# A mixture-of-experts router rebuilt: plain float32 logits on un-normed transposed rows, one block ranked at a time

## The reference, cut to what matters

```python
h = rms_norm(x, norm_ffn[l])
logits = einsum('bld,de->ble', h, router_w) + router_b
top_v, top_i = lax.top_k(logits, 2)
gates = sum(one_hot(top_i, 8) * softmax(top_v)[..., None], axis=-2)
for e in range(8):
    out = out + gates[..., e:e+1] * swiglu(h, wg[e], wu[e], wd[e])   # 1024 -> 2816 -> 1024
x = x + out
```

## Time and profile before

| | |
|---|---|
| median of 3 runs | 1372.85 us (1372.64 to 1375.06) |
| profiled execution, its own time | 1368.11 us |
| its span, first to last instruction | 1366.3 us |
| busy share of the span: PE, DVE, ACT, POOL | 96%, 73%, 59%, 9% |
| mean granted TensorE clock | 0.986 |
| share of PE in the chain that ended last | 91% |

### The profile page before, as it was taken

One profiled execution on the slowest core, in us unless ns is written; L12 is line 12 of the kernel. 1 busy time (PEld: TensorE's weight loads), 2 busy tenths in 40 slices (PEclk: granted clock), 3 DMA queues, 4 the chain that ended last, 5 costly groups with the idle time before them and its releaser, 6 DMA issues.

```text
span 1366.3 us, 15856 instructions
## 1 busy us (share of the span) xinstructions
PE 1312.4 (96%) x6292; PEld 1110.3 (81%) x6293; DVE 1001.6 (73%) x999; ACT 805.5 (59%) x817; POOL 119.3 (9%) x163
## 2 busy tenths in 40 slices
PE   5999999999998999979999999999999999999995
PEld 5997788888887997868888888888888888888884
DVE  5977533333335777478888988888889888888994
ACT  5545333222224465447777777777777777777771
POOL 1070200000000072020000000000000000000150
PEclk9999999999999999879999999999999999999998
DMA  9225597333332125169999999999999999999991
GB/s 317 88 74 183 188 414 275 123 123 123 123 124 84 62 78 192 47 249 395 389 389 378 385 384 383 383 388 370 389 379 383 390 369 390 390 373 371 392 343 60
DMA packets 179201, 373.71 MB, mean 274 GB/s; under 512 B 7084, under 2 KB 59748, under 8 KB 179126
## 3 DMA queue, kind: packets, MB, share of 16 engines
q1 hardware_dynamic: 167878, 335.78, 67.7%
q0 software_dynamic: 9456, 34.75, 6.8%
q10 hardware_dynamic: 1792, 2.18, 0.4%
HBM read 345.85 MB, written 26.82 MB: 273 GB/s over the span
## 4 chain that ended last, share of the span: by engine, by line
PE 91%; DVE 4%; ACT 2%; issue 1%; DMA 1%; SPq 0%; POOL 0%; DVEq 0%; POOLq 0%; ACTq 0%
PE ps L342 28%; PE ps L344 28%; PE ps L343 28%; PE ps L1548 2%; PE ps L1395 1%; DVE ext L916 1%; DVE a_lo L924 1%; PE ps L1477 1%; DVE w_lo L322 1%; ACT ext L587 1%; DMA ext<-in_norm_mix 1%; PE ps L1319 1%; PE ps L1351 1%; PE ps L1554 1%; DVE ps L952 0%
## 5 line engine op out<-in xcount | busy, mean ns | idle before, releaser
L322 DVE TENSOR_TENSOR w_lo<-raw,w_hi 128x2048 fp32r<-128x2048 f32 x317 | 725.1, 2291 | 140.6 <-ACT w_hi L633 81.0
L633 ACT ACTIVATE w_hi<-raw 128x2048 fp32r<-128x2048 f32 x264 | 506.3, 1919 | 139.2 <-PE ps L344 138.1
L342 PE MATMUL ps<-w_hi,xT_hi 128*128 128x512 f32 x704 | 279.8, 397 | 1.4 <-DVE xT_lo L1030 1.4
L344 PE MATMUL ps<-w_hi,xT_lo 128*128 128x512 f32 x704 | 274.9, 390 | 0.0
L343 PE MATMUL ps<-w_lo,xT_hi 128*128 128x512 f32 x704 | 274.2, 389 | 0.0
L344 PEld LDWEIGHTS ps<-w_hi,xT_lo 128*128 128x128 f32 x704 | 132.1, 188 | 28.6
L342 PEld LDWEIGHTS ps<-w_hi,xT_hi 128*128 128x128 f32 x704 | 132.3, 188 | 27.3 <-DVE xT_lo L1030 1.6
L343 PEld LDWEIGHTS ps<-w_lo,xT_hi 128*128 128x128 f32 x704 | 132.4, 188 | 26.1
L342 PE MATMUL ps<-w_hi,a_hi 128*128 128x512 f32 x360 | 141.1, 392 | 5.1 <-DVE a_lo L1130 3.0
L344 PE MATMUL ps<-w_hi,a_lo 128*128 128x512 f32 x360 | 140.3, 390 | 0.0
L343 PE MATMUL ps<-w_lo,a_hi 128*128 128x512 f32 x360 | 140.2, 389 | 0.0
(11 more groups left out here) (192 smaller groups left out, 1525.4 us busy)
## 6 DMA issues: line engine op xcount, KB each, us to landing
raw<-in_moe_w_down SPq DMA_DIRECT2D x88, 1024.0 KB, 7.5
raw<-in_moe_w_gate SPq DMA_DIRECT2D x80, 1024.0 KB, 7.3
raw<-in_moe_w_up SPq DMA_DIRECT2D x80, 1024.0 KB, 7.3
raw<-in_w_in SPq DMA_DIRECT2D x12, 1024.0 KB, 9.5
x_rows<-ext POOLq DMA_DIRECT2D x6, 2048.0 KB, 24.8
raw<-in_dense_w_gate SPq DMA_DIRECT2D x11, 1024.0 KB, 5.3
raw<-in_dense_w_up SPq DMA_DIRECT2D x11, 1024.0 KB, 5.4
raw<-in_dense_w_down SPq DMA_DIRECT2D x11, 1024.0 KB, 5.0
```

The costliest lines, as they stand in the source:

```text
L322: dve.tensor_tensor(slot(w_lo, s), slot(raw, s), slot(w_hi, s).bitcast(F32), ALU.subtract)\
L342: pe.matmul(out, lh, rh, start=start, stop=False)
L344: return pe.matmul(out, ll, rh, start=False, stop=stop)
L633: act.activation(slot(w_hi, s), slot(raw, s), ACT.Copy).then_inc(hi_ready[s], 1)
```

## The change

- **Logits.** The transposes take x before the norm (`pe_xT`), ACT copies the first two blocks to SBUF and DVE the third (`xt`), with no split. The router's weights are multiplied by the norm's gain once (`rw`; the gain arrives with the other per-channel parameters, one more small load at the start). The logits are 8 plain float32 matmuls of 8 columns per block, and 1/rms comes in as a scalar when DVE adds the bias.
- **Order on PE.** The first block's transposes, then half of the third block's last `w_out` part, the second block's transposes, a quarter, the second block's logits, the last quarter, the third block's transposes, the logits of the first and third blocks, 14 transposes of the identity into a bank that nobody reads (`keep_warm`), the counting, 10 more of these, the gather.
- **Order on ACT and DVE.** Tiles 2 and 3 are split ahead of the second block's residual add, tiles 4 and 5 on ACT ahead of the gather; on DVE tile 4 comes behind the gathered rows and tile 5 behind the gates. The ranking is one call per block (`route`), with one comparison pair and one weight table (`side`). The one-hot comes ahead of the counts and `posb`, the maximum for the softmax, the exponentials and the gates behind them.
- **Start of expert 0.** Its first tile waits only for the first half of the gathered rows; the gather's second half waits for the counts to be read.

```diff
+LOGIT_ORDER = [1, 0, 2]
+LOGIT_BANK = [7, 6, 2]
...
-        rw_hi = place("rw_hi", KD * NE, F32R)
-        rw_lo = place("rw_lo", KD * NE, F32R)
+        rw = place("rw", KD * NE)
...
+        xt = place("xt", KD * TOK, offset=oh)
...
-        low = place("low", NE * NE, offset=s0 + 512)
+        side = place("side", 2 * NE * NE, offset=s0 + 4096)
...
-        cmp_gt = place("cmp_gt", NTB * NE * NE, offset=s0 + 1024)
-        cmp_eq = place("cmp_eq", NTB * NE * NE, offset=s0 + 1792)
+        cmp = place("cmp", 2 * NTB * NE * NE, offset=s0 + 1024)
...
+        PRM_ROWS.append((C_NF, a["norm_ffn"][LAYERS - 1].rearrange("(k p) -> k p", p=P)))
...
+        def act_xT(act, i):
+
+            for half in range(2):
+                act.wait_ge(S["ht_done"], ht_count(3, i, half))
+                act.activation(ht_view(xt, TB_ORDER[i], half), ht_psum(TB_ORDER[i], half), ACT.Copy)\
+                   .then_inc(S["xt_act"], 1)
...
-                if l:
-                    act.wait_ge(S["rw_loaded"], 16)
-                    act.activation(rw_hi[:, :], rw_raw[:, :], ACT.Copy).then_inc(S["rw_hi_ready"], 1)
...
-                act_hT(act, n + 1, 0)
-                act_square(act, n + 1, 1)
-                act_square(act, n + 1, 2)
-                act_hT(act, n + 1, 1)
-                act_hT(act, n + 1, 2)
...
+                else:
+                    act.wait_ge(S["wout_used"], 3)
+                    expert_hi(act, MAIN[0], 2)
+                    expert_hi(act, MAIN[0], 3)
+                    act_xT(act, 0)
+                    act_square(act, n + 1, 1)
+                    act_xT(act, 1)
+                    act_square(act, n + 1, 2)
...
             first = MAIN[0]
-            act.wait_ge(S["wout_used"], 3)
-            expert_hi(act, first, 2)
-            expert_hi(act, first, 3)
+            act.wait_ge(S["y_blk"], NTB * LAYERS)
+            expert_hi(act, first, 4)
+            expert_hi(act, first, 5)
+            expert_xT(act, 0, 0)
             act.wait_ge(S["lg_ready"], 1)
             for tb in range(NTB):
                 act.activation(gate[:, tb * NE:(tb + 1) * NE], lg[:, tb * NE:(tb + 1) * NE], ACT.Exp,
                                bias=rmax[:, NTB + tb:NTB + tb + 1]).then_inc(S["exp_done"], 1)
-            act.wait_ge(S["wout_used"], 4)
-            expert_hi(act, first, 4)
-            expert_xT(act, 0, 0)
-            expert_hi(act, first, 5)
...
-                    dve.wait_ge(S["rw_hi_ready"], 1)
-                    dve.tensor_tensor(rw_lo[:, :], rw_raw[:, :], rw_hi[:, :].bitcast(F32), ALU.subtract)\
-                       .then_inc(S["rw_lo_ready"], 1)
+                    dve.wait_ge(S["rw_loaded"], 16)
+                    g = prm[:, C_NF:C_NF + KD].unsqueeze(2).to_broadcast([P, KD, NE])
+                    dve.tensor_tensor(rw[:, :].rearrange("p (k e) -> p k e", e=NE),
+                                      rw_raw[:, :].rearrange("p (k e) -> p k e", e=NE), g, ALU.mult)\
+                       .then_inc(S["rw_ready"], 1)
...
-                dve_hT(n, 0)
-                add(1)
-                mean_square(n, 1)
-                norm_row(n, 1)
-                add(2)
-                mean_square(n, 2)
-                dve_hT(n, 1)
-                norm_row(n, 2)
-                dve_hT(n, 2)
...
             expert_lo(MAIN[0], 2)
-            dve.wait_ge(S["logits_done"], 1)
+            expert_lo(MAIN[0], 3)
+            add(1)
+            mean_square(3, 1)
+            norm_row(3, 1)
             dve.memset(mask[:, NTB * NE:(NTB + 1) * NE], 0.0)
...
+            def add_half(dh):
+                o = x[:, TB_ORDER[2] * D + dh * 512:TB_ORDER[2] * D + dh * 512 + 512]
+                dve.tensor_tensor(o, o, ps[:, OUT_BANK[TB_ORDER[2]] + dh, :], ALU.add).then_inc(S["x_added"], 1)
+            dve.wait_ge(S["y_half"], 1)
+            add_half(0)
+            dve.wait_ge(S["y_blk"], NTB * LAYERS)
+            add_half(1)
+            for half in range(2):
+                dve.wait_ge(S["ht_done"], ht_count(3, 2, half))
+                dve.tensor_copy(ht_view(xt, TB_ORDER[2], half), ht_psum(TB_ORDER[2], half)).then_inc(S["xt_dve"], 1)
+            mean_square(3, 2)
             dve.wait_ge(S["rb_loaded"], 16)
...
+            def route(place, i):
+
+                tb = TB_ORDER[i]
+                own = lg[:, tb * NE:(tb + 1) * NE]
+                pair = cmp[:, 2 * tb * NE * NE:2 * (tb + 1) * NE * NE]
+                pair4 = pair.rearrange("p (e h j) -> p e h j", h=2, j=NE)
+                dve.wait_ge(S["rstd_ready"], NTB * 3 + i + 1)
+                dve.wait_ge(S["logits_done"], place + 1)
+                link(dve.scalar_tensor_tensor(out=own, in0=ps[:, LOGIT_BANK[i], 0:NE],
+                                              scalar=stat[:, 6 + tb:7 + tb], in1=rb[:, :], op0=ALU.mult, op1=ALU.add))
+                each = own.unsqueeze(1).to_broadcast([P, NE, NE])
+                own3 = own.unsqueeze(2).to_broadcast([P, NE, NE])
+                dve.tensor_tensor(pair4[:, :, 0], each, own3, ALU.is_ge)
+                link(dve.tensor_tensor(pair4[:, :, 1], each, own3, ALU.is_gt))
+                link(dve.tensor_tensor(pair, pair, side[:, :], ALU.mult))
+                link(dve.tensor_reduce(rank[:, tb * NE:(tb + 1) * NE],
+                                       pair.rearrange("p (e j) -> p e j", j=2 * NE), AXX, ALU.add))
+                dve.tensor_scalar(mask[:, tb * NE:(tb + 1) * NE], rank[:, tb * NE:(tb + 1) * NE], 2.0, None,
+                                  ALU.is_lt).then_inc(S["mask_ready"], 1)
+            for place, i in enumerate(LOGIT_ORDER):
+                route(place, i)
+            norm_row(3, 2)
+            dve.wait_ge(S["mask_ready"], NTB)
+            dve.wait_ge(S["iota_loaded"], 16)
+
+            dve.wait_ge(S["pos_done"], 1)
+            link(dve.tensor_scalar(post[:, :], ps[:, 3, 0:NTB * NE], float(CH), None, ALU.mult))
             for tb in range(NTB):
...
+                ins = dve.tensor_scalar(onehot[:, tb * P:(tb + 1) * P], iota, post[:, tb * NE:tb * NE + 1],
+                                        mask[:, tb * NE:tb * NE + 1], ALU.is_equal, ALU.mult)
+            ins.then_inc(S["onehot_ready"], 1)
+            link(dve.tensor_scalar(cnt_f[:, 0:NE], ps[:, 3, NTB * NE:(NTB + 1) * NE], float(CH), None, ALU.mult))
+            link(dve.tensor_reduce(cnt_f[:, NE:NE + 1], cnt_f[:, 0:NE], AXX, ALU.max))
+            dve.tensor_copy(cnt_i[:, :], cnt_f[:, :]).then_inc(S["cnt_ready"], 1)
+            link(dve.scalar_tensor_tensor(out=post[:, :], in0=post[:, :], scalar=1.0, in1=mask[:, 0:NTB * NE],
+                                          op0=ALU.add, op1=ALU.mult))
...
-            link(dve.tensor_tensor(gate[:, :], gate[:, :], mask[:, 0:NTB * NE], ALU.mult))
...
+            link(dve.tensor_reduce(rmax[:, 0:NTB], lg[:, :].rearrange("p (t e) -> p t e", e=NE), AXX, ALU.max))
+            dve.tensor_scalar(rmax[:, NTB:2 * NTB], rmax[:, 0:NTB], -1.0, None, ALU.mult).then_inc(S["lg_ready"], 1)
...
+            expert_xT(0, 0)
+            expert_lo(MAIN[0], 4)
+
+            dve.wait_ge(S["exp_done"], NTB)
+            link(dve.tensor_tensor(gate[:, :], gate[:, :], mask[:, 0:NTB * NE], ALU.mult))
...
-            expert_lo(MAIN[0], 3)
-            expert_lo(MAIN[0], 4)
-            expert_xT(0, 0)
             expert_lo(MAIN[0], 5)
...
+            def pe_xT(i):
+
+                tb = TB_ORDER[i]
+                for half in range(2):
+                    pe.wait_ge(S["x_added"], 12 + 2 * i + half + 1)
+                    for k in range(4 * half, 4 * half + 4):
+                        ins = pe.transpose(ps[:, ht_bank(tb, half), (k % 4) * P:(k % 4 + 1) * P],
+                                           x[:, tb * D + k * P:tb * D + (k + 1) * P], ident[:, :])
+                    ins.then_inc(S["ht_done"], 1)
...
+            def logits(i):
+
+                tb = TB_ORDER[i]
+                for k in range(KD):
+                    if k % 4 == 0:
+                        if i < 2:
+                            pe.wait_ge(S["xt_act"], 2 * i + k // 4 + 1)
+                        else:
+                            pe.wait_ge(S["xt_dve"], k // 4 + 1)
+                    o = k * TOK + tb * P
+                    ins = pe.matmul(ps[:, LOGIT_BANK[i], 0:NE], xt[:, o:o + P], rw[:, k * NE:(k + 1) * NE],
+                                    start=k == 0, stop=k == KD - 1)
+                ins.then_inc(S["logits_done"], 1)
+
+            def keep_warm(n):
+
+                for _ in range(n):
+                    pe.transpose(ps[:, 5, 0:P], ident[:, :], ident[:, :])
+
...
-                pe.wait_ge(S["x_lo_ready"], 2 * it.n + 2)
+                opens = it.done is None and it.n == 0
+                pe.wait_ge(S["x_lo_ready"], 1 if opens else 2 * it.n + 2)
                 for c in range(NX):
                     if c < 5:
                         expert_in(it, c, "g0")
+                        if c == 0 and opens:
+                            pe.wait_ge(S["x_lo_ready"], 2)
...
```

(47 more changed lines are left out.)

75 lines of the change are left out of this document (35 added, 40 removed).

## The result

The changed kernel takes 1356.94 us (median of 4 runs, 1354.91 to 1357.47) against 1373.09 us for the kernel before on the same chip (4 runs, 1372.64 to 1375.06): ratio 0.9885, 95% interval 0.9867 to 0.9903, 16.2 us less. The forecast was 1360.7 us with a range of 1355.4 to 1364.2. The profiled execution after took 1357.47 us, its span is 1355.6 us, its mean granted clock 0.990.

What follows compares the result with a forecast made beforehand. PE was taken to bound the expert stage, so an earlier expert 0 start ends the kernel earlier: 17.5 - 0.8 (expert 0) - 4.5 (clock) = 12.2 us, 1355.9 profiled, plus 4.7 for the median: 1360.7 us, range 1355.4 to 1364.2.

Steps and rivals of the forecast that it cites:

- the forecast case: Router stage: the clock falls once, near 572, costing 4.5 us; gain 12.2 us, 1360.7 us; chance 0.60.
- the rival in which the clock holds: Router stage: early identity transposes prevent any clock fall; gain 16.7 us, 1356.2 us; chance 0.20.
- PE bounds the expert stage: Expert stage: PE is busy for all 720 us, so starting expert 0 1 us earlier ends the kernel 1 us earlier.
- given back in expert 0: Expert 0: DVE splits and gates behind the start delay the first activation product; -0.8 us, bounds 0 and 2.3.
- PE up to the logits: Router stage, from 558.68: a block's logits are 16 instructions, 1.8 us; last logits end at 572.6; part worth 9.9 us.
- What must be ready: Ahead of the logits: tile 3 subtracted by 559.9, second block's add ends at 561.1, 1.1 us before PE wants it.
- Ranking, counting, one-hot: Behind the logits: last block's ranking 1.5 us, mask at 574.2; gains of 1.4, 0.9 and 1.2 us at full clock.
- The clock: Router stage: falls once at 572, returns after nine gather instructions; costs 4.5 us, bounds 3.0 and 6.5.
- 586 to 588: Start of expert 0: sign that its first wide product comes at this time, against a `w_out` end near 568.
- The padding does nothing: Router stage: identity transposes do not bring the clock back, half clock into the gather; gain 10.3 us, 1362.5; chance 0.08.
- DVE becomes the late one: Ahead of the logits: late subtraction of tiles 2 and 3 makes the second block's add hold PE; 1361.9 to 1364.2; chance 0.06.
- Half clock throughout: From the first logits group on, the clock stays at half through the gather; slower, about 1375.5 us; chance 0.02.

Runs made afterwards that it cites:

- the second profile of before: The kernel before, run and profiled once more with no edit: 1373.14 us (10 runs) against 1372.32, ratio 1.0007.
- the second profile of after: The changed kernel, run and profiled once more with no edit: 1357.03 us, ratio 0.9881.
- tile 4 first: The changed kernel with DVE's split of expert 0's tile 4 ahead of the split of the gathered rows: 1356.89 us, ratio 0.9878.
- the spread order: The changed kernel with its three logits groups apart, 4 + 4 more identity transposes around the last block's transposes, and ranking as logits arrive: 1354.72 us, ratio 0.9867.
- the split of tile 3 late: The changed kernel with DVE's split of tile 3 put back behind the split of the expert's rows, ahead of tile 4's: 1361.81 us, ratio 0.9916.
- the 14 + 10 alone: Logits groups apart, with the changed kernel's 14 + 10 identity transposes but without the 4 + 4 ahead of the last logits: 1356.55 us, ratio 0.9884.

## Why the prediction held, step by step, and where it was off

The mechanism was the one forecast, and most terms came out as worked out. That the time lies inside the stated range is in part luck: 1356.94 is below the forecast case's own range (1359.2 to 1362.7), and inside the whole one only by its lower end, which was taken from the rival in which the clock holds. It did not hold. The differences below are after minus forecast, on the forecast's clock (3.10 taken off).

- *PE bounds the expert stage*: right. From the first wide product to the end of the span it is 766.9 us before, 767.1 in the second profile of before, 767.8 after. The 0.7 between the last two is the "given back in expert 0", forecast as 0.8; with the second profile of after, 767.5, it is 0.4. DVE starts the first activation product 14.3 us after the start (602.15), forecast 14.4, and PE's wait there grew from 0.50 us to 1.17.
- *PE up to the logits*: float32 at 8 columns is 16 instructions a group at 0.11. The last logits end at 572.7; forecast 572.6.
- *What must be ready*: DVE's split of tile 3 ends at 559.9, as forecast, and the second block's add 1.2 us ahead of PE's need (1.1). This cover held.
- *Ranking, counting, one-hot*: the last block's ranking takes 1.47 us (1.5), the mask is there at 574.6 (574.2), since the two rankings ahead of it did not quite fit: DVE starts the last one 0.4 us later than laid out. The padding, not the ranking, releases the counting, as forecast for a fallen clock, and hides that.
- *The clock* is the term that was mis-sized. Against the 581.9 worked out for the full clock, the first product came at 584.7: 2.8 us for the fall, where I took 4.5 (bounds 3.0 to 6.5). The sign "586 to 588", given on the forecast's clock, was missed by 1.3 us. I placed the fall 13.3 us into the stage and the return after nine of the gather's instructions (580.3 and 9 x 0.22), so 10.3 us at half; it fell 14.7 us in and stayed for 6.8. The forecast case does occur: with tile 4 first the profiled execution fell 12.9 us in, for 10.2, and its stage is 27.68 us against the 27.7 of the forecast. Six profiles share PE's order up to the end of the logits; in them the fall came 12.9 to 14.8 us into the stage and lasted 3.4, 6.8 or 10.2 us. That "the clock falls once" is right for this order in all six; that it has to is wrong, since the spread order holds it.
- *The profiled execution and the runs*: I carried the 4.7 us between them over to the result. The two profiles of before are 4.9 apart (1371.2 - 1366.3): 3.37 ahead of the stage, in work that both kernels share, and 0.2 behind it, but 1.36 in the stage itself (42.07 against 40.71), and that went with it.

The sum between two profiles of typical executions: 16.03 in the stage (42.07 - 26.04), less 0.70 in expert 0, plus 0.27 ahead of the stage, is 15.6, as the spans say (1371.2 - 1355.6). Against the 12.2 forecast, 1.7 come from the clock's term, 1.4 from the short profile, 0.3 from ahead of the stage, 0.1 from expert 0. The measured 1356.94 lies nearer to the rival in which the clock holds (1356.2) than to the forecast; in both profiles after it did not hold, and the nearness comes from the two mis-sized terms.

*Rivals.* "The padding does nothing" falls in the spread order, where the padding is worth 2.6 us between medians (2.3 by the ratios) and no run without it is as fast as the slowest with all of it. In the changed kernel's own order it is not decided, as the run without padding shows. The Trainium skill, "TensorE: Matmul & The Clock Gate", Part 4 (PE-mode transpose), on which that rival leaned, says that the full clock does not engage for transposes. The trace disagrees: with the split of tile 3 late, PE ran nothing but identity transposes and eight counting products from 574.77 to 578.81, and the clock rose to 1.00 at 578.5; and the spread order held 1.00 from 573.74 to the gather with no wide product, where the same order without padding fell. What is left of the rival: in the changed kernel's order, where the clock fell inside the logits, the padding did not bring it back sooner and cost 0.84 us. "DVE becomes the late one" did not occur: the second block's add kept its 1.2 us, and no run took them away, so the price of that rival stays untested. The late split moves DVE's work to the other end, behind the gather. "Half clock throughout" and the lost gain did not occur.

Open stays why executions of one kernel differ (the changed kernel's eight runs by 2.8 us, the kernel before's by 6.2 in one group, 1368.27 to 1374.47): in the kernel before the mean clock goes with the time (0.986 at 1368.27, 0.979 at 1374.47), in the changed one it need not (0.990 at 1357.47, 0.986 at 1357.43), and only the profiled ones show where it fell.

## What to carry to other kernels

When a stage of narrow work and waits lies between wide products, count not only what is on the path but what TensorE does in each wait: here identity transposes in the waits, together with narrow groups laid between wide ones, kept the clock at full in all three profiles that had the groups apart and transposes in both waits behind the last logits. With the groups together, or with those waits empty, it fell in every profile. One trace is one execution, though: two of the four runs with the 14 + 10 alone were 2 us slower than the one profiled. Before sizing a gain on one profile, compare that execution's time with the runs' median, and where they differ find the stretch that differs: it may be the one you remove. A queue that releases the first wide work after such a stage (here DVE's splits) is worth clearing early, since a wait of 3.3 us there cost its own length and, in the one profile of it, a clock fall within it that slowed the products behind.

## What the runs showed of the hardware

In the one profile with a wait of 3.33 us in expert 0, PE had run wide products back to back at 1.00 before it; the clock fell within the wait and was at half for 3.4 us, most of them under wide products again. In seven profiles with 1.1 to 1.2 us at the same place it did not fall. And where layer 1 begins, in identical code, the clock was at half for 3.4 us in one profile, 6.8 in three and 10.2 in nine: the same work does not get the same clock each time.
